# Expert tiles of a two-model chain on Trainium2: taken two at a time from the seventh on, with the overflow tiles spread among the fixed ones

## The reference

```python
pg = jax.nn.softmax(t @ wgc + bgc)           # 4 groups
gw, gi = lax.top_k(pg, 1)
tv, ti = lax.top_k(jax.nn.softmax(fs), 2)    # fs: the 4 logits of the chosen group
tv = tv / jnp.sum(tv, axis=-1, keepdims=True)
eid = gi * EXPERTS_PER_GROUP + ti            # two of 16 experts, of one group
act = jax.nn.silu(t @ w1[e]) * (t @ w3[e]) * gates[e]   # 1024 -> 256
y += act @ w2[e]                                         # 256 -> 1024
```

## Time and profile before

| what | value |
|---|---|
| median of three runs | 2746.53 us |
| the profiled execution | 2741.5 us |
| its span | 2739.5 us |
| PE busy | 2681.4 us, 98% of the span |
| DVE, ACT, POOL busy | 1772.4, 1090.2, 1597.1 us |
| mean granted TensorE clock | 0.989 |
| longest waits of PE for DVE's `hactT` | 4.8 us in 5 waits |

### The profile page before, as it was taken

How to read it: one execution, slowest core, us unless ns; L and a number is a source line. 1 busy time by engine, 2 the same in 40 slices (tenths; PEclk the granted TensorE clock), 3 DMA queues, 4 the chain that set the end, 5 groups by cost and what they waited for, 6 DMA issues and landing times. The chain is left out here.

```text
span 2739.5 us, 35274 instructions
## 1 busy us (share of the span) xinstructions
PE 2681.4 (98%) x12337; PEld 2093.5 (76%) x12337; DVE 1772.4 (65%) x2575; ACT 1090.2 (40%) x1892; POOL 1597.1 (58%) x979
## 2 busy tenths in 40 slices
PE   8999999999999999999999989999999999999998
PEld 6777778888887777788888877778777677787675
DVE  6787755444127787654444749886777588777775
ACT  3844423222025544432221011644556415545554
POOL 5754466666676744486666765576236555772263
PEclk9999999999999999999999989999999999999999
DMA  4332222333332312223333322236896232357951
GB/s 156 86 84 62 63 86 83 96 96 100 92 93 85 100 62 70 62 85 94 98 97 126 109 90 85 70 100 241 303 354 209 69 97 73 94 209 295 352 181 64
DMA packets 89673, 340.29 MB, mean 124 GB/s; under 512 B 21568, under 2 KB 24384, under 8 KB 80064
## 3 DMA queue, kind: packets, MB, share of 16 engines
q1 hardware_dynamic: 66592, 298.02, 32.9%
q0 software_dynamic: 19008, 26.28, 3.7%
q10 hardware_dynamic: 3936, 14.16, 1.4%
HBM read 368.77 MB, written 33.55 MB: 147 GB/s over the span
## 5 line engine op out<-in xcount | busy, mean ns | idle before, releaser
L188 POOL TENSOR_TENSOR wl<-ring,wh 128x1024 fp32r<-128x1024 f32 x317 | 784.0, 2473 | 26.4
L186 POOL TENSOR_SCALAR wh<-ring 128x1024 fp32r<-128x1024 f32 x317 | 352.0, 1111 | 724.1 <-PE ps L265 516.5
L263 PE MATMUL ps<-xh,wh 128*128 128x512 f32 x1592 | 633.8, 398 | 14.0 <-DVE xl L1421 11.8
L264 PE MATMUL ps<-xl,wh 128*128 128x512 f32 x1592 | 621.2, 390 | 0.0
L265 PE MATMUL ps<-xh,wl 128*128 128x512 f32 x1592 | 621.2, 390 | 0.0
L263 PEld LDWEIGHTS ps<-xh,wh 128*128 128x128 f32 x1592 | 299.6, 188 | 94.2 <-issue 12.6
L265 PEld LDWEIGHTS ps<-xh,wl 128*128 128x128 f32 x1592 | 299.6, 188 | 64.2
L264 PEld LDWEIGHTS ps<-xl,wh 128*128 128x128 f32 x1592 | 300.0, 188 | 60.8 <-issue 1.0
L1673 DVE SCALAR_TENSOR_TENSOR taps<-ps,par,taps 128x511 f32<-128x511 f32 x192 | 143.8, 749 | 232.1 <-ACT taps L1391 216.3
L3271 DVE TENSOR_TENSOR ew_l<-ew,ew_h 128x1024 fp32r<-128x1024 f32 x184 | 214.1, 1217 | 5.2 <-ACT ew_h L2794 5.1
L2794 ACT ACTIVATE ew_h<-ew 128x1024 fp32r<-128x1024 f32 x184 | 180.6, 1050 | 13.3 <-DMA ew<-in_eu 9.3
(11 more groups left out here) (628 smaller groups left out, 5326.0 us busy)
## 6 DMA issues: line engine op xcount, KB each, us to landing
ring<-in_w SPq DMA_DIRECT2D x343, 512.0 KB, 3.6
ew<-in_eu SPq DMA_DIRECT2D x32, 2048.0 KB, 12.5
ew<-in_ed SPq DMA_DIRECT2D x32, 1024.0 KB, 11.4
xrows<-xr ACTq DMA_DIRECT2D x8, 512.0 KB, 2.8
yrows<-xr ACTq DMA_DIRECT2D x8, 512.0 KB, 3.8
yg<-yrows SPq DMA_DIRECT2D x8, 512.0 KB, 5.1
z<-in_x SPq DMA_DIRECT2D x4, 512.0 KB, 5.7
join_in<-in_ln ACTq DMA_DIRECT2D x1, 2048.0 KB, 9.4
```

The source lines that it names most:

```text
L186: nc.gpsimd.tensor_scalar(hi, raw, 1.0, 0.0, ALU.mult, ALU.add).then_inc(sem["w_hi"], 1)
L188: nc.gpsimd.tensor_tensor(lo, raw, hi, ALU.subtract).then_inc(sem["w_split"], 1)
L263: nc.tensor.matmul(out, wh, xh, start=first, stop=False, **kw)
L264: nc.tensor.matmul(out, wh, xl, start=False, stop=False, **kw)
```

## The change

`TWINS` = 6. Tiles 0 to 5 run as before. Tiles 6 to 21 run in eight pairs (6, 7) to (20, 21), tile 22 alone. A pair's turn on PE is two up products, the activation turns of tiles j-1 and j in one go, the row turns of tiles j+2 and j+3, and the down products of j-1 and j. The second tile of a pair has buffers of its own for its transposed rows (`xgT_h1`, `xgT_l1`) and turns them in PSUM banks 2 and 7; the down product of the first goes to banks 0 and 1; `hact` is doubled, and `hactT` holds two tiles and is copied at once. Overflow tiles are now tiles 4, 7, 10, 13, 16, 19 and 22 (`is_spare`), so the two filled ones of layer 0 are tiles 4 and 7, the filled one of layer 1 is tile 4. A scatter waits for the one before it when either is of an overflow tile.

```diff
+TWINS = 6
+def is_twin(j):
+    return TWINS <= j < TILES - 1 and j % 2 == 0
+def is_spare(j):
+    return j > EW_BUFS and j % EW_BUFS == 1
 def held(j):
-    return j % GROUPS * (EXPERTS // GROUPS) + j // GROUPS if j < EXPERTS else j
+    fixed = j - spares_until(j)
+    return EXPERTS + spares_until(j) if is_spare(j) else fixed % GROUPS * (EXPERTS // GROUPS) + fixed // GROUPS
...
@@ POOL
-                        if j >= EXPERTS:
+                        if j and (is_spare(j) or is_spare(j - 1)):
                             g.wait_ge(sem[f"y_out{(j - 1) % 2}"], at(f"y_out{(j - 1) % 2}", 16 * ((j - 1) // 2 + 1)))
...
+                    for j in range(TWINS):
+                        if is_spare(j + EW_BUFS):
+                            spare_up(j + EW_BUFS)
+                        gather_rows(j + 3)
+                        if j and is_spare(j + EW_BUFS - 1):
+                            spare_down(j + EW_BUFS - 1)
+                        if j:
+                            scatter_rows(j - 1)
+                    gather_rows(TWINS + 3)
+                    for j in range(TWINS, TILES - 1, 2):
...
+                        for i in (j, j + 1):
+                            if i + EW_BUFS < TILES and is_spare(i + EW_BUFS):
+                                spare_up(i + EW_BUFS)
+                        for i in (j, j + 1):
+                            if i + 4 < TILES:
+                                gather_rows(i + 4)
+                        for i in (j - 1, j):
+                            if i + EW_BUFS < TILES and is_spare(i + EW_BUFS):
+                                spare_down(i + EW_BUFS)
+                            scatter_rows(i)
...
@@ PE
+                    for j in range(TWINS):
                         expert_up(j)
                         if j:
                             turn_hidden(j - 1)
-                        if j and j + 1 < TILES:
                             turn_rows(j + 1)
-                        if j:
+                            if j == TWINS - 1:
+                                turn_rows(j + 2)
                             expert_down(j - 1)
+                    for j in range(TWINS, TILES - 1, 2):
+                        expert_up(j)
+                        expert_up(j + 1)
+                        turn_hidden(j - 1, j)
+                        turn_rows(j + 2)
+                        if j + 3 < TILES:
+                            turn_rows(j + 3)
+                        expert_down(j - 1)
+                        expert_down(j)
+                    expert_up(TILES - 1)
+                    turn_hidden(TILES - 2)
+                    expert_down(TILES - 2)
...
@@ ACT
+                    for j in range(TWINS, TILES - 1, 2):
+                        if j > TWINS:
+                            y_evac(j - 2)
+                        weights_high(j + 1, (UP_PARTS - 1,))
+                        gate_silu(j)
+                        weights_high(j + 2, range(UP_PARTS))
+                        gate_silu(j + 1)
+                        turn_evac(j + 2)
+                        if j + 3 < TILES:
+                            turn_evac(j + 3)
+                        y_evac(j - 1)
+                        if j + 3 < TILES:
+                            weights_high(j + 3, range(UP_PARTS - 1))
...
@@ DVE
+                    for j in range(TWINS, TILES - 1, 2):
+                        if j > TWINS:
+                            y_evac(j - 2)
+                        weights_low(j + 1, (UP_PARTS - 1,))
+                        gated_hidden(j)
...
+                        weights_low(j + 2, range(UP_PARTS - 1))
+                        scaled_token(j)
+                        hidden_evac(j - 1, j)
+                        gated_hidden(j + 1)
+                        turn_evac(j + 2)
+                        if j + 3 < TILES:
+                            turn_evac(j + 3)
+                        weights_low(j + 2, (UP_PARTS - 1,))
+                        y_evac(j - 1)
+                        if j + 3 < TILES:
+                            weights_low(j + 3, range(UP_PARTS - 1))
+                        scaled_token(j + 1)
+                    y_evac(TILES - 3)
+                    gated_hidden(TILES - 1)
+                    hidden_evac(TILES - 2)
+                    y_evac(TILES - 2)
```

More of the change, by code:

```diff
@@ L1737, in turns_of, with turns_until, spares_until @@
     return len(range(k, n, of))
+def is_twin(j):
+    return TWINS <= j < TILES - 1 and j % 2 == 0
+def turns_until(j):
+    return j + 1 if j < TWINS - 1 else j + 1 - (min(j, TILES - 3) - (TWINS - 1) + 1) // 2
+def is_spare(j):
+    return j > EW_BUFS and j % EW_BUFS == 1
+def spares_until(j):
+    return sum(is_spare(i) for i in range(j))
 def held(j):
-    return j % GROUPS * (EXPERTS // GROUPS) + j // GROUPS if j < EXPERTS else j
+    fixed = j - spares_until(j)
+    return EXPERTS + spares_until(j) if is_spare(j) else fixed % GROUPS * (EXPERTS // GROUPS) + fixed // GROUPS
 PER2 = {"w_split": U2, "unit_done": U2, "z_ready": C8, "x_ready": 2 * C8, "xa_ready": 2 * C8, "xh_ready": 2 * C8, "par_in2": 16, "tab_in": 32,
@@ L1824, in second_block @@
         sil = at_("sil", 152, [P, DE])
-        hact = at_("hact", 153, [P, DE])
-        hactT = at_("hactT", 154, [P, EC, P])
+        hact_of = (at_("hact", 153, [P, DE]), at_("hact1", 196.75, [P, DE]))
+        hactT = at_("hactT", 154, [P, 2 * EC, P])
         xr = at_("xr", 156, [P, 4, D])
@@ L1884, in second_block, with turned_second, turn_bank, down_bank @@
         ident = con("ident")
-        def turn_bank(j):
-            return 0 if j else 4
+        def turned_second(j):
+            return 1 if j > TWINS and j % 2 else 0
+        def turn_bank(j, half):
+            if turned_second(j):
+                return 7 if half else 2
+            return half if j else 4 + half
+        def down_bank(j):
+            return 0 if is_twin(j) else 5
         def hy_unit(j):
@@ L2087, in spare_up @@
                     def spare_up(j):
-                        k, last = j - EXPERTS, (layer + 1) * ROWS_E - 1
+                        k, last = spares_until(j), (layer + 1) * ROWS_E - 1
                         for half, name in enumerate((f"es_ua{k % 2}", f"es_ub{k % 2}")):
@@ L2121, in _ @@
                     gather_rows(2)
-                    for j in range(TILES):
+                    for j in range(TWINS):
[8 more added lines that the diff above has]
+                    for j in range(TWINS, TILES - 1, 2):
                         if layer + 1 < DEPTH and j in NEXT_AT:
@@ L2520, in expert_up, with turn_hidden @@
                             mm.then_inc(sem["up_mm"], 1)
-                    def turn_hidden(j):
-                        pe.wait_ge(sem["hact"], at("hact", j + 1))
-                        for f in range(EC):
-                            mm = T.transpose(ps[:, 4, f * P:f * P + P], hact[:, f * P:f * P + P], ident)
+                    def turn_hidden(*tiles):
+                        for i, j in enumerate(tiles):
+                            pe.wait_ge(sem["hact"], at("hact", j + 1))
+                            for f in range(EC):
+                                to = (EC * i + f) * P
+                                mm = T.transpose(ps[:, 4, to:to + P], hact_of[j % 2][:, f * P:f * P + P], ident)
                         mm.then_inc(sem["hactt_mm"], 1)
@@ L2543, in expert_down @@
                                 a_ = EW_UP + f * D + half * S
-                                mm = T.matmul(ps[:, 5 + half, :], hactT[:, f, :], ew[:, b, a_:a_ + S], start=(f == 0), stop=(f == EC - 1))
+                                mm = T.matmul(ps[:, down_bank(j) + half, :], hactT[:, EC * is_twin(j) + f, :], ew[:, b, a_:a_ + S],
+                                              start=(f == 0), stop=(f == EC - 1))
                             mm.then_inc(sem["dn_mm" if half else "dn_half"], 1)
-                    for j in range(TILES):
+                    for j in range(TWINS):
                         expert_up(j)
@@ L2799, in turn_evac @@
                         for half in halves:
[L2800 removed]
+                            A(xgT_h_of[turned_second(j)][:, 4 * half:4 * half + 4, :],
+                              ps[:, turn_bank(j, half), :].rearrange("p (k t) -> p k t", t=P), ACT.Copy
                               ).then_inc(sem["xgt_hi"], 1)
@@ L2807, in y_evac, with gate_silu @@
                             act.wait_ge(sem[f"y_out{j % 2}"], at(f"y_out{j % 2}", 16 * (j // 2)))
-                        A((y_b if j % 2 else y_a)[:, 0:S], ps[:, 5, :], ACT.Copy).then_inc(sem["y_lo"], 1)
+                        A((y_b if j % 2 else y_a)[:, 0:S], ps[:, down_bank(j), :], ACT.Copy).then_inc(sem["y_lo"], 1)
+                    def gate_silu(j):
+                        act.wait_ge(sem["up_mm"], at("up_mm", UP_PARTS * (j + 1)))
+                        act.wait_ge(sem["hact"], at("hact", j))
+                        A(sil[:, :], ps[:, 2 + j % 2, 0:DE], ACT.Silu).then_inc(sem["silu"], 1)
```

(5 more changed lines are left out.)

129 lines of the change are left out of this document (75 added, 54 removed).

## The result

The changed kernel takes 2778.48 us, median of five runs (2772.81 to 2779.39), against 2746.53 (2745.39 to 2746.92) before: the medians differ by 32 us. I had forecast 2751.8 in a range of 2745 to 2757. The sign leaned the right way; the size was off by a factor of six. The profiled execution is 2772.81 us with a span of 2770.8, 31.3 more than before; the mean granted clock fell from 0.989 to 0.984.

What follows compares the result with a forecast made beforehand. The prediction took PE's instructions to bound the kernel (busy 2681.4 of 2739.5 us). Pairs -2.0, stage end +1.3, tile 7's gather +4.9 and clock +1.1 make +5.3 on 2746.5: 2751.8 us, range 2745.0 to 2757.0.

Steps and rivals of the forecast that it cites:

- the +1.3: End of both expert stages: DVE does `hact` of tile 22 first, so tile 21's down product is 0.64 us later, twice.
- my 2.5 to 6.3: Layer 0, row turn of tile 7: PE waits 2.5 to 6.3 us for its gather, taken as 4.9.
- Later gathers have about a pair less one row turn and are safe.: Gathers after that of tile 7: enough time to land, so no wait of PE.
- The clock after a wait, +1.1: Behind the wait for tile 7's gather in layer 0: PE runs at half clock for a while, costing 1.1 us.
- The other edits cost nothing.: Pair loads, empty overflow tiles, the next-layer weight split on POOL and the move of `spread_last`: no cost.
- DVE and ACT should not hold a pair up.: In the pairs: DVE has 9.7 us of splits in 20, some 16 with evacuations, so no cost.
- the 20.2: Pairs, activation turn to activation turn: longer than 20.2 us would mean DVE, ACT or a scatter holds them; 20.0 expected.
- my +5.3: Whole kernel: sum of the terms, -2.0 + 1.3 + 4.9 + 1.1 us, added to the median before.
- pairs -0.3 (-2.0): Expert stages of both layers: the -2.0 is the forecast gain of pairs, 1.1 us in layer 0 and 0.9 in layer 1.
- no wait: Rival, tile 7 in layer 0: its gather lands in under 9 us and PE does not wait, 2745.8 us; chance 0.13.
- the whole ring: Rival, tile 7 in layer 0: gather takes 17.5 us behind its ring, PE waits 8.6 us, 2755.8 us; chance 0.18.
- the chain of scatters: Rival, pairs near overflow tiles: scatters waiting for each other cost 4.2 us a pair, two pairs, 2760.2 us; chance 0.08.

Runs made afterwards that it cites:

- pairs-only kernel: The changed kernel with the overflow tiles back at places 16 to 22 (also called pairs alone): 2759.60 us, ratio 1.0045.
- tile 21 empty: The changed kernel with overflow tile 5 (counted from 0) at place 21 in place of 19: 2768.26 us, ratio 1.0081.
- pairs alone, mended: The pairs-only kernel with the gather of tile 9 ahead of tile 4's scatter and, on DVE, `hactT` of tile 21 first: 2752.21 us, ratio 1.0026.
- half loads later: The changed kernel with both half loads of tile 4 held until the up product of tile 1 is done: 2774.96 us, ratio 1.0109.
- the last two runs: First: pairs alone, mended with tile 7's rows turned after tile 4's down product, 2745.06 us; second: that, POOL's next-layer splits at tiles 14 and 16, 2747.37 us.
- the mended kernel: The changed kernel with gathers of tiles 7 and 9 first, tile 4's half loads later, tile 21 empty, `hactT` of tile 21 first: 2746.23 us, ratio 1.0002.

## Why the prediction was wrong

**What held.** The kernel is bound by PE. Pairs take 19.96 to 20.0 us and give about 1 us a layer (layer 1: 175.39 - 170.88 - 3.71 of wait - 1.70 of clock = -0.9, as forecast). Tile 21's down product waits 1.10 us and not 0.52 in both layers, near the +1.3. The rows of tile 7 come late in layer 0, 2.84 us, at the low end of my 2.5 to 6.3, and not in layer 1.

**"Later gathers have about a pair less one row turn and are safe."** This step failed and cost the most: 4.10 + 3.71 us of wait. I counted from when the buffer of tile 9 comes free. I did not read what stands ahead of that gather on POOL's program, although the change puts it last in turn 5: a down load waiting for tile 4's down product, and a scatter. Moved ahead, the waits were gone in both layers. In the pairs-only kernel, where only the scatter stands there, the wait was 0.40 and 3.03.

**The clock after a wait, +1.1.** Half clock came behind the two waits that I had not forecast, and not behind the one that I had: after 2.84 us the granted clock stayed at 1.00, and the turn lost 0.2. The pair with the wait of 4.10 us took 26.96, so 26.96 - 19.97 - 4.10 = 2.9 us more; that with 3.71 took 25.38, 1.7 more. So 4.8 us in all. I had bounded this loss by half clock over one stretch of 3.4 us, after the earlier trace rows; after 4.10 it lasted 6.8. And the length of a wait does not settle it: 2.69 us (tile 21 empty) and 2.84 were followed by full clock, but 2.70 (pairs alone, mended), 2.80 (pairs alone) and 2.97 (half loads later) by 3.4 us of half clock, which cost 1.9 each.

**"The other edits cost nothing."** This step failed twice. Spreading puts a fixed expert with rows at place 21, whose scatter the `yg` loads wait for: +3.3 us a layer from scatter to load. And it issues the first half load of tile 4 at 1939.50, 2.0 us before the end of the up product of tile 1, beside SP's load of tile 3, where the splits and `hactT` of tile 1 were already close: +2.4 and +1.4 us. With both halves later 1.8 of the one and all of the other were gone. Both sit at the ends of the stage. I looked at its middle, where PE was covered.

**"DVE and ACT should not hold a pair up."** Two pairs in layer 0 took 21.01 and 20.66, 1.7 us together, over the 20.2 that I had named as a sign of being wrong. In the changed kernel it begins with ACT, which waits 8.32 us for the half load of tile 13 behind POOL's split for the next layer; DVE's splits come late by that but are not longer (3.50 and 3.49 us). This is read from the trace, and no run moves that half load ahead. In the pairs-only kernels, which have no such half load, the last two runs put the long pairs down to the same splits of POOL in another way: DVE's take longer beside them. In the kernel before, POOL's splits at 2035 and 2055 lengthen no turn (10.28 us at the first, 10.29 at the same place of layer 1 without them, and 10.02 at the second).

Against my +5.3: gathers 10.7 (forecast 4.9), clock 4.8 (1.1), end of stage 7.1 and tile 1 3.7 (both 0), `hactT` of tile 21 1.2 (1.3), pairs -0.3 (-2.0). That is 27.1 before rounding; 3.6 between the stages, not of the change, and 0.6 in the first and last line of the table make 31.3. Of the rivals, "no wait" was false, the whole ring too (2.84 us of wait and not 8.6), and the chain of scatters never decided: the undisturbed pairs are at 19.96 to 19.99. (The scatter of the earlier trace rows is that of tile 10, not 11.)

The two profiled executions differ by 3.6 us in a part that the change does not touch, yet the medians differ by 32.0, so some 4 us of the medians' difference have no place in this table. Ten runs of the mended kernel at 1.0002 say that the mended terms together make up all of it within about 3 us; the size of each is read from single profiles.

## What to carry to other kernels

When a change makes something needed a turn earlier, follow its request through the program of the engine that issues it: what stands ahead, and what does that wait for? Reordering one line there was worth more here (12.5 us) than the whole change could give (2.0). And look at both ends of a stage: an order that is free in the middle decides there which transfer is the last one that somebody waits for. A reordering whose best case is 2 us of 2746 has many more ways to lose than to win; with all of them mended, neither the pairs nor the whole change is measurably faster than the kernel before.

## What the runs showed of the hardware that I had not expected

Half clock with a busy PE. In the stretch from 2285.70 above PE is busy 3.40 of 3.40 us and the granted clock is 0.51. The changed kernel has the same in the same place of its program:

```profile
2300.70:2304.10 3.40, 3.40 (x10) 2.71 (x9) 3.33 (x5) 0.59 (x2) 1.09 (x1) 0.50 0.25 58
```

The kernel before had one stretch of half clock between the stages in one profile (at 2351.03) and three in the other. What makes them come and go was not tried and stays open. Runs of one kernel spread over 10 us here, and they go with the mean granted clock: of 31 runs of the kernel before on one chip, the five at 0.989 and 0.990 took 2741.05 to 2744.04 us, the fifteen at 0.986 and 0.987 took 2744.28 to 2751.85. That it is such stretches which make the difference is argued, not shown.

A scatter with accumulation that has rows holds back the waiting load 6.2 us, an empty one 2.9 (2.8 with the tile made empty again), with the DMA engines' share at 0.35 and 0.05 meanwhile, so the engines were full in neither case. A gather of one tile's rows took from under 9.2 to 15.1 us from issue to use, by what else was in flight.
